# Roots of two norms applied behind the products instead of ahead of them

## The reference, cut to what matters

```python
def _rmsnorm(x, g):
    y = xf * lax.rsqrt(jnp.mean(xf * xf, axis=-1, keepdims=True) + EPS)
    return y * g
...
    h = h + mixed @ w_out[l]
    h = h + _memory_cross_attention(_rmsnorm(h, norm_xattn[l]), _rmsnorm(mem, norm_mem[l]), w_xq[l], w_xkv[l], w_xo[l])
    h = h + _hierarchical_moe(_rmsnorm(h, norm_ffn[l]), w_router_group[l], ..., w_gate, w_up, w_down)
...
def _memory_cross_attention(hn, mn, w_xq, w_xkv, w_xo):
    q = (hn @ w_xq).reshape(b, s, N_XATTN_HEADS, XATTN_HEAD_DIM)
    logits = jnp.einsum('bshd,bmhd->bhsm', q, k) * (XATTN_HEAD_DIM ** -0.5)
...
def _hierarchical_moe(u, ...):
    p_group = softmax(t @ w_rg + b_rg)
    e_logits = t @ w_re + b_re
    for e in range(N_EXPERTS):
        hidden = jax.nn.silu(t @ w_gate[e]) * (t @ w_up[e])
        y = y + gate[:, e:e + 1] * (hidden @ w_down[e])
```

## Time and profile before

| | us |
|---|---|
| median of three timed runs | 1632.14 |
| the profiled execution's own time | 1625.92 |
| its span in the trace | 1624.1 |
| mean granted TensorE clock | 0.995 of full |
| PE busy | 1559.8 (96%) |
| DVE busy | 1060.2 (65%) |
| ACT busy | 762.3 (47%) |

### The profile page before, as it was taken

One profiled execution on the slowest core, in us unless ns is written; L12 is line 12 of the kernel. 1 busy time (PEld: TensorE's weight loads), 2 busy tenths in 40 slices (PEclk: granted clock), 3 DMA queues, 4 the chain that ended last, 5 costly groups with the idle time before them and its releaser, 6 DMA issues.

```text
span 1624.1 us, 27286 instructions
## 1 busy us (share of the span) xinstructions
PE 1559.8 (96%) x9955; PEld 1370.4 (84%) x9955; DVE 1060.2 (65%) x1794; ACT 762.3 (47%) x1309; POOL 99.5 (6%) x165
## 2 busy tenths in 40 slices
PE   8999999999999999999899999999999998999997
PEld 7998788899999997875677888888887895899997
DVE  5577486788888879624755655555557846765564
ACT  5544544544444454444643641145224365665562
POOL 0011000000000000000300100010000001000000
PEclk9999999999999999999999999999999999999999
DMA  8666054487777733330331654455442452256552
GB/s 301 207 227 200 28 194 158 126 283 246 256 239 241 248 110 108 103 91 13 66 107 63 216 197 135 145 186 196 157 152 76 136 131 39 68 156 192 171 192 90
DMA packets 71497, 253.86 MB, mean 156 GB/s; under 512 B 7888, under 2 KB 11120, under 8 KB 71168
## 3 DMA queue, kind: packets, MB, share of 16 engines
q1 hardware_dynamic: 54048, 189.43, 35.3%
q0 software_dynamic: 17376, 63.44, 13.6%
HBM read 251.73 MB, written 1.11 MB: 156 GB/s over the span
## 4 chain that ended last, share of the span: by engine, by line
PE 84%; DVE 9%; ACT 3%; issue 3%; DMA 0%; DVEq 0%; SPq 0%; ACTq 0%
PE pair L1095 83%; ACT wh L585 1%; DVE uv L1775 1%; PE pair L1139 1%; DVE sq L2313 1%; DVE sq L1815 1%; DVE small L1807 1%; DVE wl L1734 1%; PE pair L1274 1%; ACT sq L653 0%; DVE spent L1867 0%; DVE uh_f L1867 0%; DVE ul L1764 0%; DVE res L2466 0%; DMA table<-in_table 0%
## 5 line engine op out<-in xcount | busy, mean ns | idle before, releaser
L1095 PE MATMUL pair<-uh,wh 128*128 128x256 f32 (+3 forms) x1864 | 581.8, 312 | 11.6 <-DVE ul L1764 5.5
L1734 DVE TENSOR_TENSOR wl<-ring,wh 128x1024 fp32r<-128x1024 f32 x350 | 427.1, 1224 | 248.3 <-ACT wh L585 242.2
L1095 PE MATMUL pair<-uh,wl 128*128 128x256 f32 (+3 forms) x1864 | 577.4, 310 | 0.0
L1095 PE MATMUL pair<-ul,wh 128*128 128x256 f32 (+3 forms) x1864 | 576.3, 309 | 0.0
L585 ACT ACTIVATE wh<-ring 128x1024 fp32r<-128x1024 f32 x350 | 367.4, 1052 | 260.6 <-PE pair L1095 253.4
L1095 PEld LDWEIGHTS pair<-uh,wh 128*128 128x128 f32 (+1 forms) x1864 | 346.6, 186 | 40.4 <-issue 13.4
L1095 PEld LDWEIGHTS pair<-ul,wh 128*128 128x128 f32 (+1 forms) x1864 | 346.3, 186 | 23.4
L1095 PEld LDWEIGHTS pair<-uh,wl 128*128 128x128 f32 (+1 forms) x1864 | 346.6, 186 | 23.0
L1095 PE MATMUL pair<-hh,wh 128*128 128x512 f32 (+1 forms) x512 | 172.9, 338 | 0.8
L1095 PE MATMUL pair<-hh,wl 128*128 128x512 f32 (+1 forms) x512 | 172.2, 336 | 0.0
L1095 PE MATMUL pair<-hl,wh 128*128 128x512 f32 (+1 forms) x512 | 172.2, 336 | 0.0
(11 more groups left out here) (279 smaller groups left out, 1983.8 us busy)
## 6 DMA issues: line engine op xcount, KB each, us to landing
ring<-in_w_stream SPq DMA_DIRECT2D x350, 512.0 KB, 3.8
uh_f<-in_mods POOLq DMA_DIRECT2D x48, 512.0 KB, 6.2
mod_w<-in_mods POOLq DMA_DIRECT2D x48, 512.0 KB, 3.8
uv<-c_rows POOLq DMA_DIRECT2D x4, 512.0 KB, 6.6
ml<-ml_dram POOLq DMA_DIRECT2D x4, 512.0 KB, 8.3
table<-in_table SPq DMA_DIRECT2D x1, 1849.5 KB, 12.0
res<-in_x SPq DMA_DIRECT2D x4, 256.0 KB, 4.1
res<-in_mem SPq DMA_DIRECT2D x1, 1024.0 KB, 14.3
```

The costliest lines, as they stand in the source:

```text
L1095: ins = pe.matmul(*operands, **flags)
L1734: tt(wl[:, s, :], ring[:, s, :], wh[:, s, :].bitcast(F32), ALU.subtract).then_inc(S("w_lo"), 1)
```

## The change: the roots behind the products

For the norms `xattn` and `ffn` DVE no longer waits for `rstd`. As soon as a job has been added to `res`, it multiplies its two tiles by the gain only (`xv`, `fv`), ACT rounds them (`xh`, `fh`), DVE takes the rest (`xl`, `fl`), in buffers of their own. PE multiplies these. The sum of squares moves behind the first three pieces of `xq` in PE's list, and behind tile 5 of the router logits. The `turn_over` matmuls of both norms are gone. The root is multiplied on: onto the queries (`query`, DVE, in place of ACT's copy), the router logits (DVE, in place of ACT), the gate product of every half expert (`scale_gate`, new, 32 times) and the gate weights, which covers the up product. Two modulation tiles move from `out1` to `xq`.

```diff
-SPIN = {"mix": (0, 19, 6), "sb": (0, 6, 6), "xattn": (6, 8, 6), "ffn": (6, 8, 6),
+SPIN = {"mix": (0, 19, 6), "sb": (0, 6, 6),
...
-MOD_OUT, MOD_XQ, MOD_XAT, MOD_XO = 4, 4, 0, 2
+MOD_OUT, MOD_XQ, MOD_XAT, MOD_XO = 2, 6, 0, 2
...
# ACT
-            def added_squares(name, phase, first):
+            def added_squares(name, phase, first, hi, v):
                 for t in range(4):
                     split(first + 2 * t + 1 + AHEAD - (t == 3))
                     wait_emptied(act, phase, t)
                     square(name, t, res[:, 2 * t:2 * t + 2, LAT], P, 512)
+                    for k in (2 * t, 2 * t + 1):
+                        round_u(name, k, [(hi[:, k, :], v[:, k, :], None)])
                 split(first + 7 + AHEAD)
                 root(name, P, T, D)
-            added_squares("xattn", "out1", S_OUT)
-            round_tiles("xattn", LAT)
+            added_squares("xattn", "out1", S_OUT, xh, xv)
             for s in range(4):
                 split(S_XQ + 2 * s + 1 + AHEAD)
-                b = full(act, "xq", s)
-                emptied(act.activation(qx[...], b[...], ACT.Copy, scale=256 ** -0.5), "act")
...
-                act.wait_ge(S("moe_gate"), i * UNIT_TURN + (a + 1))
-                act.activation(eg[:, a % 2, :], bank[4 + a % 2][:, 0:T], ACT.Silu).then_inc(S("moe_silu"), 1)
+                act.wait_ge(S("moe_scaled"), i * UNIT_TURN + (a + 1))
+                act.activation(eg[:, a % 2, :], eg[:, a % 2, :], ACT.Silu).then_inc(S("moe_silu"), 1)
# PE
-            norm("xattn", P, T)
-            linears("xq", S_XQ, LAT, "xattn")
+            linears("xq", S_XQ, slice(0, T), "xattn", lambda: norm("xattn", P, T), (xh, xl))
...
-            norm("ffn", P, T)
-            few_rows(S_RT, rt_bank, LAT, "ffn").then_inc(S("rt_logits"), 1)
+            few_rows(S_RT, rt_bank, slice(0, T), "ffn", (fh, fl), lambda: norm("ffn", P, T)).then_inc(S("rt_logits"), 1)
# DVE
+            def query(s):
+                b = full(dve, "xq", s)
+                dve.wait_ge(S("norm_rstd"), NORM["xattn"] + 1)
+                emptied(stt(qx[...], b[...], 256 ** -0.5, rstd[...], ALU.mult, ALU.mult), "dve")
 def add_to_res(...):
                     emptied(tt(r, b[...], r, ALU.add), "dve")
+                    dve.wait_ge(S("job_emptied_dve"), JOBS.emptied(JOBS.number(phase, s))[1])
+                    for k in (2 * s, 2 * s + 1):
+                        ts(v[:, k, :], res[:, k, LAT], tab(gain)[:, k:k + 1], None, ALU.mult).then_inc(S("u_v"), 1)
+                    for k in (2 * s, 2 * s + 1):
+                        rest(name, k, [(lo[:, k, :], v[:, k, :], hi[:, k, :], None)])
...
-            norm_tiles("xattn", res, "g_xattn", LAT, LAT)
             for s in range(4):
                 split(S_XQ + 2 * s + 1 + AHEAD)
-                if s < MOD_XQ:
-                    mod_tiles(1, spent[:, :, :])
+                if s:
+                    query(s - 1)
+                mod_tiles(2 if s in (0, 3) else 1, spent[:, :, :])
+            query(3)
...
+            dve.wait_ge(S("rt_logits"), 1)
+            dve.wait_ge(S("norm_rstd"), NORM["ffn"] + 1)
+            ch.link(tt(logit_rows[0:20, :], rt_bank[0:20, 0:T], rstd[0:20, 0:T], ALU.mult))
+            ts(logit_rows[0:20, :], logit_rows[0:20, :], tab("b_route", 20), None, ALU.add).then_inc(S("rt_rows"), 1)
             add_squares("ctx", 512)
...
+            def scale_gate(i, a):
+                dve.wait_ge(S("moe_gate"), i * UNIT_TURN + (a + 1))
+                tt(eg[:, a % 2, :], bank[4 + a % 2][:, 0:T], rstd[:, 0:T], ALU.mult).then_inc(S("moe_scaled"), 1)
...
                 if k >= 0:
+                    scale_gate(i, a)
                     split_turn(i, N_TURN, S_MOE, p + 3, p + 3)
```

More of the change, by code:

```diff
@@ L136, in normed @@
 def normed(name):
+    if name == "xattn":
+        return JOBS.emptied(JOBS.number("xq", 3))
     if name in V_N:
@@ L786, in _ @@
             root("ctx", P, T, D, rstd[:, T:2 * T])
-            split(S_MOE + 3)
-            act.wait_ge(S("gate_full"), 1)
-            act.activation(logit_rows[0:NE, :], rt_bank[0:NE, 0:T], ACT.Copy).then_inc(S("gate_rows"), 1)
-            act.wait_ge(S("gate_two"), 1)
-            act.activation(gates[:, 0:2, :], gate_bank[:, :].rearrange("p (a t) -> p a t", a=2),
-                           ACT.Copy).then_inc(S("gate_first"), 1)
             split(S_MOE + 4)
@@ L1161, in norm, with together @@
                 turn_over(after, spare)
-            def together(ready, n, outs, ks=range(KT)):
+            def together(ready, n, outs, ks=range(KT), src=(uh, ul)):
                 if ks[0] == 0:
@@ L1174, in together @@
                             begun.append(n + j)
-                        last = prod(o, n + j, k, uh[:, k, cc], ul[:, k, cc], k == 0 and begins, k == KT - 1, m=m,
+                        last = prod(o, n + j, k, src[0][:, k, cc], src[1][:, k, cc], k == 0 and begins, k == KT - 1, m=m,
                                     skip_group_check=True)
@@ L1227, in few_rows @@
                     pe.wait_ge(S("u_l"), U_AT[ready] + k + 1)
-                    last = prod(b[:, 0:cc.stop - cc.start], n, k, uh[:, k, cc], ul[:, k, cc], k == 0, k == KT - 1)
+                    last = prod(b[:, 0:cc.stop - cc.start], n, k, src[0][:, k, cc], src[1][:, k, cc], k == 0, k == KT - 1)
+                    if then and k == 5:
+                        then()
                 return last
@@ L1406, in gate_up @@
                     for k in range(KT):
-                        last = prod(bank[4 + 2 * q + a % 2][:, 0:T], p + q, k, uh[:, k, LAT], ul[:, k, LAT],
+                        last = prod(bank[4 + 2 * q + a % 2][:, 0:T], p + q, k, fh[:, k, :], fl[:, k, :],
                                     k == 0, k == KT - 1)
@@ L2045, in _ @@
             dve.memset(modv[:, 2 * N_MOD:4 * N_MOD], 0.0).then_inc(S("macc_out"), 1)
+            dve.wait_ge(S("gate_full"), 1)
+            tt(logit_rows[0:NE, :], rt_bank[0:NE, 0:T], rstd[0:NE, 0:T], ALU.mult).then_inc(S("gate_rows"), 1)
+            scale_gate(0, 0)
+            dve.wait_ge(S("gate_two"), 1)
+            tt(gates[:, 0:2, :], gate_bank[:, :].rearrange("p (a t) -> p a t", a=2),
+               rstd[:, 0:T].rearrange("p (a t) -> p a t", a=1).to_broadcast([P, 2, T]), ALU.mult).then_inc(S("gate_first"), 1)
             split(S_MOE + 4)
```

42 lines of the change are left out of this document (23 added, 19 removed).

## The result

The changed kernel takes 1648.69 us in the median (1646.50 to 1649.53, 4 runs), the kernel before on the same chip 1631.33 (1629.22 to 1632.33, 4 runs): ratio 1.0106, 95% interval 1.0089 to 1.0124. That is +17.4 us, or 1.1%, slower, where the forecast was 1643.8, +11.7 over 1632.1. The profiled execution took 1649.5 (span 1647.7).

What follows compares the result with a forecast made beforehand. PE, busy 96% of the span, was taken as the bound, so a change pays only where PE waits. 12.9 + 1.3 + 3.4 - 5.9 + 0 = +11.7 us over 1632.1 gave 1643.8 us, range 1636 to 1652.

Steps and rivals of the forecast that it cites:

- a fall at the router: PE's wait of about 2 us for the router logits may lower its clock: 0 to +1.7 us, taken as 0.
- Part 1: out1 on DVE: 1.7 us added per job, two modulation tiles removed; xq begins at 224.0 instead of 225.79 us.
- Part 2: Queries: ACT's root holds the fourth xq split, DVE idles 10.6 us, scores begin at 262.2 against 249.33: +12.9 us.
- Landing: Modulation tiles following each other directly in two places wait for their buffers to be loaded anew: +1.3 us.
- Part 3: TensorE's clock falls once at together and once at the scores, after waits without constant matmuls: +3.4 us, bounds 0 and 6.8.
- Part 4: Experts' norm: PE turns the logits at 302.0 instead of 307.89 us, then as before: -5.9 us.
- Part 5: scale_gate in the experts' loop: 32 DVE instructions of about 0.4 us fit in DVE's free time: 0.
- The head start: Rival at the queries: fourth xq split not held by the root, scores 2.2 us late, 1628.4 us, faster; 6%.
- Costs smaller throughout: Rival for the whole kernel: PE's list hides more of DVE's costs, near no change, 1632 to 1636 us; 4%.
- the experts' loop slips: Rival in the experts' loop: DVE's new wait holds each unit by 0.2 to 0.4 us, +6 to +13, about 1653; 6%.
- the clock stays up and the tiles land early: Rival around the queries: no clock loss and no landing waits, +7.0 us, 1639.1 us; 20%.

Runs made afterwards that it cites:

- the mended kernel: Changed kernel with ACT's two splits ahead of the root, last query earlier, DVE's first xq split one piece shorter, one tile from out1 to xo: 1637.8 us, ratio 1.0037.
- the kernel with the last query first: Changed kernel with DVE's last query product ahead of the last two modulation tiles of xq, not behind them: 1637.7 us, ratio 1.0052 to the kernel before.

## Why the prediction was right, and which terms were off

The sign, the size and the mechanism of the queries held: 1648.7 lies in the range of 1636 to 1652, 5 us above the forecast. Part of the agreement is luck: the stages add up to +11.6 against +11.7 because the scores came 1.6 us less late than forecast and a fall at the router, priced at 0, cost 1.6. By its own steps:

- **Part 1, `xq` from 224.0.** In before's time (3.42 taken off) `xq` begins at 223.89. The steps from addition to addition on DVE held to 0.1 us (6.94, 5.21 and 4.11 for 7.0, 5.3 and 4.1). Its last step is written as 4.3 where its terms add up to 4.2.
- **Part 2, +12.9.** Right in place and size, and only in part in its cause. Sum of squares 234.0 (forecast 232.5 and the fall's 1.7 = 234.2), root 235.9 (236.1), DVE's block 25.8 us long (25.3), idle 11.9 (10.6 + 1.7). The scores came +14.3 late where +15.9 was forecast in all, for no tile landed late (1.3), and DVE began 0.4 earlier: root's end at 235.4 and a split of 1.04 give 236.4, not the 236.8 of the text. The cause that it names, the root ahead of the fourth piece's split, holds for 3 of the idle 11.9 us. The rest is the ring place, which PE gives free only at the end of `together` and which the prediction doesn't mention. The number came out because the two are over within 3 us of each other; that was luck.
- **Landing, +1.3.** 0 in the first trace, 2.81 in the second, 2.90 and 1.01 in relatives. A value in the middle (half of 2.8 is 1.4) was a fair price for something that comes and goes.
- **Part 3, the clock, +3.4.** Two falls on the path, as said. 1.4 in `together` (the constant matmuls gave back 1.3) and 2.1 at the scores (5.84 against 3.72 for 16 matmuls), of which the stage behind shows at most 1.7. There were four and not two on the way, and the other two lay under DVE's work. That taking `turn_over` out is what costs didn't hold: with more constant matmuls than the kernel before has, three of the four falls were gone, and the scores came 0.3 us earlier; the fourth came all the same. The fall at the router, costed at 0 with a bound of 1.7, came in four of the ten traces with the changed router of that order and cost 1.5 each time.
- **Part 4, -5.9.** -5.94, and within 0.04 of it in eight more traces of kernels with this norm and router and two tiles in `xo`.
- **Part 5, 0.** Right for what it costed: the loop has no wait, and taking the multiplication out changed nothing in it. The part that failed is one that the sum takes without a word, that PE's matmuls in the loop take what they took before. The loop costs 3.2 us more through the tile that they read.
- **Rivals.** The head start was to decide at one point, "whether ACT's fourth `xq` split runs before the root". Moved there, it gave 1.3 us of the stage, not 10: the same split waits on the place of a used piece. This rival's 1628.4 had no way to come true. "Costs smaller throughout" and "the experts' loop slips" by DVE's wait are out. Of "the clock stays up and the tiles land early" the second half came true in the first trace; the clock fell.

The forecast was +11.7 and the medians differ by 17.4. The stages give 11.6 of it and the loop 3.2. The other 2.6 isn't tied down: a tile that lands up to 3 us late in other executions than the first can be in it, and falls of the clock outside the changed stages. Those are 8.2 us more in the trace after than in the one before, belong to neither kernel for certain, and explain the traces' 23.6, not the medians' 17.4.

Still open: up to 3 us of the mended kernel's loss, why the kernel with the last query first has fewer falls of the clock, and what about a tile's place in memory sets the spacing of the matmuls.

## What to carry to other kernels

Work that is moved behind a later event takes with it what stands behind it in the queues of the other engines: here a root in ACT's list, two filler tiles of DVE behind a split that had to wait and two more ahead of the last query made most of 14.3 us, and putting them in order, with one tile moved to a stage that had room, brought 12.5 back with the arithmetic unchanged. Before a head start is counted, list every wait of the instruction that should run early, the free place in a ring too, and not only its order; the profile before the change may already show that wait. And where two kernels differ by many clock falls, compare from mark to mark in one stage; a whole time hides what an edit did.

## What was not expected of the hardware

- With the gate and up products' moving operand in one tile 20 us of the loop hold 171 matmuls and a weight load takes 188 ns, with it in another 169 and 192 ns, at the same shape and whatever the layout. That is 1.2% of a loop that only PE bounds (8.64 us a unit against 8.54).
- A fall of the granted clock to half cost 1.3 us in `xq`'s first products, 1.5 behind the router, and 1.7 to 2.1 in the 16 score matmuls (5.41 and 5.84 for 3.72), and nothing that shows under another engine's work. It followed waits of PE of 1.78 to 11.35 us, but not each of them: behind the same wait of 1.78 us at the router it came in four of ten traces. Constant matmuls that end 2.16 us before the real ones didn't prevent it.
- Executions of one kernel have their falls at different places. On one chip six runs of the changed kernel had mean clocks of 0.985 to 0.991 and differ by 6 us (1644.5 to 1650.5), and 23 of the one before had 0.987 to 0.996 and differ by 11 (1625.4 to 1636.4).
